# Rotating queries and keys in the projection's PSUM banks, with the order of the attention and mixing stage rewritten

## The reference

```python
h = rms_norm(x, norm1_g)
ua, qb, kb, vb, qc, kc, vc, gc = split(h @ w_in)      # 256, 3 x 512, 4 x 256 columns
ya = rms_unit(s5_mixer(ua, ...))                      # state space scan, gelu, sigmoid gate
yb = rms_unit(moba_mixer(qb, kb, vb, gq, gk, cos, sin))   # 8 heads of 64, causal softmax
yc = retention_mixer(qc, kc, vc, gc, cos, sin)        # 4 heads of 64, rotated over all 64
x = x + (concat(ya, yb, yc) * mix_out_g) @ w_out
x = x + peer_layer(rms_norm(x, norm2_g), ...)         # top 16 of 16384 experts in 8 heads
```

## Time and profile before

| | us |
|---|---|
| median of 3 runs | 957.19 |
| lowest and highest | 955.43, 958.66 |
| the profiled execution, its own time | 956.8 |
| span of the profiled execution | 955.0 |
| TensorE busy | 922.6 |
| VectorE busy | 695.2 |
| ScalarE busy | 539.0 |
| GpSimd busy | 427.1 |

### The profile page before, as it was taken

The page is one execution under the profiler, slowest core; times in us unless marked ns, Lnnn a source line. Parts: engine busy times, 40 slices in busy tenths (PEclk is TensorE's granted clock), DMA queues, the critical chain, the costliest instruction groups (busy, mean ns, idle before and its releaser), DMA issues.

```text
span 955.0 us, 20048 instructions
## 1 busy us (share of the span) xinstructions
PE 922.6 (97%) x5920; PEld 831.6 (87%) x5920; DVE 695.2 (73%) x1523; ACT 539.0 (56%) x1060; POOL 427.1 (45%) x340
## 2 busy tenths in 40 slices
PE   7797789999999999999999999999999999999998
PEld 6575578999999999999999999888888888888886
DVE  7679641107999702888888886888888888888886
ACT  7374554655554564555555555665655655565653
POOL 4583226778888888777777777100000000000000
PEclk9899799999999999999999999999999999999999
DMA  9542205045666666555565655776767767776673
GB/s 334 186 171 95 78 11 199 1 153 181 232 227 226 231 225 204 199 203 195 189 197 189 199 196 192 245 248 229 250 242 236 247 232 248 244 234 242 239 245 128
DMA packets 67739, 191.53 MB, mean 201 GB/s; under 512 B 6656, under 2 KB 8576, under 8 KB 67712
## 3 DMA queue, kind: packets, MB, share of 16 engines
q1 hardware_dynamic: 67712, 191.19, 58.8%
HBM read 173.86 MB, written 17.30 MB: 200 GB/s over the span
## 4 chain that ended last, share of the span: by engine, by line
PE 73%; POOL 11%; issue 7%; DVE 6%; ACT 2%; POOLq 0%; DMA 0%; DVEq 0%
PE ps L415 22%; PE ps L417 22%; PE ps L416 22%; POOL w_lo L1513 10%; PE ps L685 3%; DVE routing L743 2%; DVE ps L743 1%; PE ps L400 1%; ACT routing L1275 1%; POOL w_lo L1500 1%; DVE ps L894 1%; DVE small L743 0%; DVE route_t L743 0%; PE ps L407 0%; ACT w_hi L1217 0%
## 5 line engine op out<-in xcount | busy, mean ns | idle before, releaser
L1410 ACT ACTIVATE w_hi<-raw 128x512 fp32r<-128x512 f32 x512 | 308.4, 628 | 136.5 <-PE ps L417 135.7
L1513 POOL TENSOR_TENSOR w_lo<-raw,w_hi 128x512 fp32r<-128x512 f32 x256 | 327.1, 1299 | 81.3 <-ACT w_hi L1410 81.1
L415 PE MATMUL ps<-h_hi,w_hi 128*128 128x256 f32 x1088 | 308.5, 284 | 2.7 <-POOL w_lo L1513 1.4
L416 PE MATMUL ps<-h_lo,w_hi 128*128 128x256 f32 x1088 | 307.9, 283 | 0.0
L417 PE MATMUL ps<-h_hi,w_lo 128*128 128x256 f32 x1088 | 307.9, 283 | 0.0
L743 DVE TENSOR_TENSOR w_lo<-raw,w_hi 128x512 fp32r<-128x512 f32 x256 | 177.4, 693 | 56.7 <-ACT w_hi L1410 41.5
L415 PEld LDWEIGHTS ps<-h_hi,w_hi 128*128 128x128 f32 x1088 | 208.8, 192 | 3.5 <-POOL w_lo L1513 1.6
L416 PEld LDWEIGHTS ps<-h_lo,w_hi 128*128 128x128 f32 x1088 | 208.8, 192 | 0.0
L417 PEld LDWEIGHTS ps<-h_hi,w_lo 128*128 128x128 f32 x1088 | 208.8, 192 | 0.0
L415 PE MATMUL ps<-w_hi,hot_gate 128*128 128x512 f32 x512 | 199.2, 389 | 0.0
L416 PE MATMUL ps<-w_lo,hot_gate 128*128 128x512 f32 x512 | 199.2, 389 | 0.0
(11 more groups left out here) (197 smaller groups left out, 871.6 us busy)
## 6 DMA issues: line engine op xcount, KB each, us to landing
raw<-in_u_t SPq DMA_DIRECT2D x128, 512.0 KB, 3.4
raw<-in_v SPq DMA_DIRECT2D x128, 512.0 KB, 3.3
act_spill<-acts SPq DMA_DIRECT2D x62, 256.0 KB, 2.1
acts<-act_spill SPq DMA_DIRECT2D x62, 256.0 KB, 3.4
routing<-in_w_in SPq DMA_DIRECT2D x5, 2048.0 KB, 11.6
routing<-in_w_out SPq DMA_DIRECT2D x2, 2048.0 KB, 7.9
routing<-in_w_q SPq DMA_DIRECT2D x2, 2048.0 KB, 8.0
xs<-in_x SPq DMA_DIRECT2D x2, 512.0 KB, 4.3
```

The costliest lines, as they stand in the source:

```text
L415: pe.matmul(dst, s_hi, m_hi, start=first and i == 0, stop=False)
L416: pe.matmul(dst, s_hi, m_lo, start=False, stop=False)
L1410: A.activation(w_hi[:, 2 * (s % 2) + h, :], raw[:, s, h * HALF:(h + 1) * HALF], ACT.Copy)\
L1513: G.tensor_tensor(w_lo[:, slot, :], raw[:, s, h * HALF:(h + 1) * HALF], w_hi[:, slot, :].bitcast(F32), ALU.subtract).then_inc(lo_ready, 1)
```

## The change

**In PSUM.** `projected(0)` still copies the queries to SBUF; their rotation reads banks 0 and 1 and writes the rotated 16 columns into `qk`. The query's gain is folded into the cos and sin tables (`rope_q`, three small products). `projected(1)` copies the scaled keys to banks 4 and 5 instead of SBUF; squares, gain, rotation and normalisation read there, and the last multiplication writes `qk`. `projected(2)` is dropped: the retention's rotation reads banks 0 and 1, scales by `rx`, writes `ret`, and now stands in front of `states(2)`, behind a wait for slice 23.

**Waits.** Projection 2 waits for `turn_ready` 1, projection 3 also for `rot_ready`, projection 5 for `ret_rot_ready`. `drive(3)` stands in front of `late_scores(1)`, and so between slices of projection 4. `c_neg` moves behind the third scores.

**The end of the stage.** The transposes of att1's second half go through banks 4 and 5 in front of y; the first attention output also moves ahead of y. The mix parts have banks 3, 2, 4, 7, the output product has (0, 1) and (5, 6), and its first two slices start on the retention's part, ahead of `moba_mix`. The eight `keep_warm` matmuls go. On ScalarE the two lots of `exps` become one, a tiny Gelu follows them, and `root(8)`, `root(16)` come ahead of the gate's Tanh.

```diff
@@ by_slices @@
                     if k == 0 and n == 2:
-                        pe.wait_ge(turn_ready, 2)
-                    if k == 0 and n >= 3:
-                        pe.wait_ge(proj_ready, 2 * (n - 2))
+                        pe.wait_ge(turn_ready, 1)
+                    if k == 0 and n == 3:
+                        pe.wait_ge(proj_ready, 2)
+                        pe.wait_ge(rot_ready, 1)
+                    if k == 0 and n == 4:
+                        pe.wait_ge(proj_ready, 4)
+                    if k == 0 and n == 5:
+                        pe.wait_ge(ret_rot_ready, 1)
@@ TensorE's order @@
             by_slices(2, range(6, KC))
-            by_slices(3, range(0, 3))
             turn_heads(0)
-            by_slices(3, range(3, KC))
+            by_slices(3, range(0, 6))
             pe.wait_ge(states_ready, 2)
             drive(2)
-            by_slices(4, range(0, 4))
+            by_slices(3, range(6, KC))
+            by_slices(4, range(0, 1))
             turn_heads(1)
-            by_slices(4, range(4, 6))
+            by_slices(4, range(1, 3))
             late_scores(0)
+            by_slices(4, range(3, 6))
+            pe.wait_ge(states_ready, 3)
+            drive(3)
             by_slices(4, range(6, KC))
             late_scores(1)
-            by_slices(5, range(0, 2))
+            by_slices(5, range(0, 3))
...
-            by_slices(5, range(2, 4))
-            pe.wait_ge(states_ready, 3)
-            drive(3)
-            pe.wait_ge(ret_rot_ready, 1)
-            pe.wait_ge(proj_ready, 8)
+            by_slices(5, range(3, 4))
+            pe.wait_ge(proj_ready, 6)
...
+            pe.wait_ge(pT_ready, 4)
+            for b in range(2):
+                turn(4 + b, [att1[:, 4 * b + h, P:S] for h in range(4)])
+
+            pe.wait_ge(pT_ready, 6)
+            for h in range(MH):
...
+                mm = pe.matmul(ps[:, 4, c], att0[:, g // 4, g % 4, :], mv[:, 0, c], start=True, stop=True)
...
+            pe.wait_ge(ret_mix, 1)
+            transpose_mix(0)
+            out_slices(0, range(0, 2))
+            pe.wait_ge(moba_mix, 1)
+            transpose_mix(1)
+            transpose_mix(2)
             pe.wait_ge(ya_ready, 1)
...
-            keep_warm(ident, 7, 8)
...
+            out_slices(0, range(2, 6))
+            pe.wait_ge(s5_mix, 1)
+            transpose_mix(3)
+            out_slices(0, range(6, KC))
+            out_slices(1, range(KC))
@@ VectorE @@
+            def rotate(dst_, x_, m, cos, sin, turned, scales):
+
+                heads = x_[0].shape[1]
+                over = lambda a, n: a.unsqueeze(1).to_broadcast([P, heads, n])
+                for t in range(TT):
+                    did(V.scalar_tensor_tensor(turned[:, t, :, 0:m], x_[t][:, :, m:2 * m], scales[t], over(sin[:, t, 0:m], m),
+                                               ALU.mult, ALU.mult))
+                    did(V.scalar_tensor_tensor(turned[:, t, :, m:2 * m], x_[t][:, :, 0:m], scales[t],
+                                               over(sin[:, t, m:2 * m], m), ALU.mult, ALU.mult))
+                settle()
+                for t in range(TT):
+                    did(V.scalar_tensor_tensor(x_[t][:, :, 0:2 * m], x_[t][:, :, 0:2 * m], scales[t], over(cos[:, t], 2 * m),
+                                               ALU.mult, ALU.mult))
+                settle()
+                for t in range(TT):
+                    ins = tt(dst_[t], x_[t][:, :, 0:2 * m], turned[:, t], ALU.add)
...
-            step(tt(k4, k4, gain(1, 0, HD), ALU.mult))
+            k_p = psum_heads(4)
+            for t in range(TT):
+                did(tt(k_p[t], k_p[t], cols(V_GQK + HD, HD).unsqueeze(1).to_broadcast([P, MH, HD]), ALU.mult))
+            settle()
+            step(rotate([k_p[t][:, :, 0:ROPE] for t in range(TT)], k_p, half_rope, rope[:, 0], rope[:, 1], scratch(ROPE),
+                        (1.0, 1.0)))
             step(rstd_of(qk_var, 0, 32, qk_rstd))
...
-            V.tensor_scalar(c_neg, c_s, -1.0, None, ALU.mult).then_inc(c_ready, 1)
-            dve.wait_ge(c_ready, 1)
+            dve.wait_ge(half_used, 3 * KC)
+            rotate([ret[:, t, 0:2 * RW].rearrange("p (h d) -> p h d", d=HD) for t in range(TT)], psum_heads(0), HD // 2,
+                   ret_turn[:, 0], ret_turn[:, 1], scratch(HD), rx_t).then_inc(ret_rot_ready, 1)
...
             states(2)
@@ ScalarE @@
-            dst = [qk[:, :, 0:MW], qk[:, :, MW:2 * MW], ret[:, :, 0:2 * RW], ret[:, :, 2 * RW:4 * RW], mv]
+            dst = [qk[:, :, 0:MW], ps[:, 4:6, :], None, ret[:, :, 2 * RW:4 * RW], mv]
...
-            slices_high(range(16, 19))
+            slices_high(range(15, 19))
+            heads_back(0, mqT)
+            act.wait_ge(rotT_ready, 1)
             projected(1)
             square_heads(1)
...
             late_exps(0)
-            slices_high(range(34, 35))
+            projected(3)
+            slices_high(range(34, 36))
             late_exps(1)
-            projected(3)
-            slices_high(range(35, 37))
+            slices_high(range(36, 38))
...
-            exps([(att0[:, g // 4, g % 4, :], g) for g in range(4)])
-            slices_high(range(38, 39))
-            exps([(att0[:, g // 4, g % 4, :], g) for g in range(4, MH)])
-            slices_high(range(39, 40))
-            act.wait_ge(proj_ready, 8)
+            exps([(att0[:, g // 4, g % 4, :], g) for g in range(MH)])
+            A.activation(spare, quarter, ACT.Gelu_apprx_tanh)
+            act.wait_ge(proj_ready, 6)
...
+            root(8)
+            out_squares(1)
+            root(16, 8)
+            transposed_high(V_GM, 1, MIX_ORDER[0:2], MIX_BANKS, 0)
             act.wait_ge(glu_psum, 1)
             A.activation(gate_s, ps[:, 7, :], ACT.Tanh, scale=0.5).then_inc(gate_ready, 1)
-            root(8)
-            root(16, 8)
```

More of the change, by code:

```diff
@@ L288, in build @@
         std = tiny(32)
+        spare = tiny(1)
         hmax, hsum = tiny(16), tiny(16)
@@ L757, in _, with transposed_low @@
             V.memset(quarter, float(np.pi / 2)).then_inc(zeros_ready, 1)
-            def transposed_low(gain, n, order=range(KC)):
-                for i, k in enumerate(order):
+            def transposed_low(gain, n, order=range(KC), banks=range(4), first=0):
+                for i, k in enumerate(order, first):
                     dve.wait_ge(th_ready, n * KC + 2 * (i // 2) + 2)
-                    V.scalar_tensor_tensor(h_lo[:, k, :], ps[:, k // 2, (k % 2) * S:(k % 2 + 1) * S], cols(gain + k, 1),
+                    V.scalar_tensor_tensor(h_lo[:, k, :], ps[:, banks[i // 2], (i % 2) * S:(i % 2 + 1) * S], cols(gain + k, 1),
                                            h_hi[:, k, :].bitcast(F32), ALU.mult, ALU.subtract).then_inc(tl_ready, 1)
@@ L850, in _, with psum_heads, scratch @@
             dve.wait_ge(bb_ready, 1)
[L852 to L858, removed]
[L859 to L861 removed]
+            def rotate(dst_, x_, m, cos, sin, turned, scales):
[6 more added lines that the diff above has]
+                                               over(sin[:, t, m:2 * m], m), ALU.mult, ALU.mult))
+                settle()
+                for t in range(TT):
+                    did(V.scalar_tensor_tensor(x_[t][:, :, 0:2 * m], x_[t][:, :, 0:2 * m], scales[t], over(cos[:, t], 2 * m),
+                                               ALU.mult, ALU.mult))
+                settle()
+                for t in range(TT):
+                    ins = tt(dst_[t], x_[t][:, :, 0:2 * m], turned[:, t], ALU.add)
+                    if t == 0:
+                        did(ins)
+                return ins
             def by_head(a):
                 return qk[:, :, a * MW:(a + 1) * MW].rearrange("p t (h d) -> p t h d", d=HD)
+            def psum_heads(bank):
+                return [ps[:, bank + t, :].rearrange("p (h d) -> p h d", d=HD) for t in range(TT)]
+            def scratch(n, first=1024):
+                return rot_tmp[:, first:first + TT * MH * n].rearrange("p (t h d) -> p t h d", t=TT, h=MH)
+            rx_t = [rx[:, t:t + 1] for t in range(TT)]
             def head_sums(a):
@@ L932, in _ @@
                    ALU.mult))
+            half_rope = ROPE // 2
+            did(tt(rope_q[:, 0], rope[:, 0], cols(V_GQK, ROPE).unsqueeze(1).to_broadcast([P, TT, ROPE]), ALU.mult))
+            for a, b in ((0, half_rope), (half_rope, 0)):
+                did(tt(rope_q[:, 1, :, a:a + half_rope], rope[:, 1, :, a:a + half_rope],
+                       cols(V_GQK + b, half_rope).unsqueeze(1).to_broadcast([P, TT, half_rope]), ALU.mult))
             head_sums(0)
+            settle()
             q4, k4 = by_head(0), by_head(1)
-            step(tt(q4[:, :, :, 0:ROPE], q4[:, :, :, 0:ROPE], gain(0, 0, ROPE), ALU.mult))
-            rotate(q4[:, :, :, 0:ROPE], ROPE // 2, rope, rot_tmp[:, 1024:1280]).then_inc(rot_ready, 1)
+            dve.wait_ge(proj_ready, 2)
+            rotate([q4[:, t, :, 0:ROPE] for t in range(TT)], psum_heads(0), half_rope, rope_q[:, 0], rope_q[:, 1], scratch(ROPE),
```

(17 more changed lines are left out.)

142 lines of the change are left out of this document (63 added, 79 removed).

## The result

The changed kernel takes 944.54 us in the median of four runs (942.65 to 948.87), against 957.47 for the kernel before beside it: 12.9 us less, a ratio of 0.9873 with a 95% interval from 0.9836 to 0.9911. The forecast was 941.1 with a range of 935 to 949.

What follows compares the result with a forecast made beforehand. TensorE, busy 922.6 of 955.0 us, bounds the kernel; in the front VectorE's chain sets the pace. 8.3 + 2.0 + 8.7 + 2.3 - 2.7 = 18.6 us, less 2.5 for the clock: gain 16.1, 941.1 us, range 935 to 949 (own range 937 to 945).

Steps and rivals of the forecast that it cites:

- Step A: Start of projection 2: its stall and slow stretch go, `states(1)` starts at 44.5 instead of 52.78, 8.3 us gained.
- the tables and sums of q: VectorE's work between its phases and the query rotation, ahead of `states(1)`: put at 2.0 us.
- Step B: Keys on VectorE: stretch of 7.0 us instead of 12.9, `states(2)` at 66.0 against 76.33, gain 2.0 us more.
- Step C: From `states(2)` to the last projection slice: about 3.5 us new stall, end at 95.6 against 114.6, another 8.7 us gained.
- Step D: From the last projection slice to the first output slice: 23.8 us against 26.1, 2.3 gained, with a 2.6 us stall.
- the clock behind D's stall: TensorE's lower clock after the 2.6 us stall in front of the retention scores: 2.5 us lost.
- Step E: Output product: 25.5 us against 22.8, 2.7 lost, the two new table loads costed at nothing.
- Rival 1: Both new stalls have longer slow stretches behind them, small pieces and hand-overs cost more: gain 8.6, 948.6 us; chance 0.20.
- Rival 2: GpSimd is faster by some 2 us over 16 slices and the clock holds: gain 20.6, 936.6 us; chance 0.10.
- Rival 3: Gain of the early start and keys is waited away before `drive(3)` and the exponentials: under 3 us, 955 to 957; chance 0.04.
- Rival 4: TensorE stays at 1.2 GHz from `drive(3)`'s stall until the output product is done: loss 38.2, 995.4 us; chance 0.03.
- the 9 us that I had named as a sign of being wrong: On TensorE: a slow stretch longer than 9 us would show the forecast wrong.

Runs made afterwards that it cites:

- e3_keys_sbuf: Changed kernel, but the scaled keys go to SBUF and their gain, rotation and normalisation run there with the same instructions: 948.65 us, ratio 0.9917.
- e0_after: The changed kernel measured once more, nothing altered, as the mark for the other runs: 943.77 us, ratio 0.9860.
- e1: Kernel before with one edit, projection 2 waits for `turn_ready` 1 instead of 2: 948.97 us, ratio 0.9922.
- e11: Changed kernel with `turn_ready` 2 restored in front of projection 2 and the keys in SBUF: 959.53 us, ratio 1.0023.
- e2: Changed kernel with the wait for `turn_ready` 2 restored in front of projection 2: 952.27 us, ratio 0.9963.
- e5: Changed kernel with 32 small matmuls put into TensorE's stall in front of `drive(3)`: 944.87 us, ratio 0.9891.
- e4: Changed kernel with 24 small matmuls put into TensorE's stall in front of the retention scores: 945.64 us, ratio 0.9876.
- e7: Changed kernel with `drive(3)` behind `late_scores(1)` and, on ScalarE, `projected(3)` and slices 34, 35 ahead of the first exponentials: 942.57 us, ratio 0.9862.
- e6: Changed kernel with ScalarE's `projected(4)` ahead of the silu and the spare Gelu behind the last probabilities: 942.75 us, ratio 0.9844.
- e8: Changed kernel with the rearrangements of e6 and e7 together: 939.67 us, ratio 0.9828.

## Why the prediction was right, and by how much it was off

The sign and the path were right: 12.9 us where 16.1 were forecast, and 944.54 lies inside both ranges that were stated. Step by step, in the profiled execution, with its late start of 2.2 us taken off:

**Step A** (start at 44.5, 8.3 us gained): `states(1)` at 46.1, 6.6 gained. The stall went as said. What failed is the 2.0 us for "the tables and sums of q": that stretch took 3.7 us (42.63 to 46.33). The 48-element product takes 1.16 us, the three `rope_q` products, which I had put at nothing, 1.49. They have two operands in SBUF while GpSimd runs, which is the very price that step B counted for the keys and step A forgot. The same 48-element product took 0.21 us in the kernel before, where GpSimd stood still from 39.03 to 44.15 us (first line); the second is GpSimd's in the changed kernel:

```profile
40.46 0.21 DVE L743 TENSOR_TENSOR vec<-vec 128x48 f32<-128x48 f32 x1
...
39.51 5.47 POOL L1557 TENSOR_TENSOR w_lo<-routing,w_hi 128x512 fp32r<-128x512 f32 x4 [2.31 <-ACT w_hi L1270]
```

`drive(1)` was not what was waited for: its last matmul ends at 46.71 us, 1.6 us before `states(1)` starts. The early start alone is worth 7.7 us on the chip.

**Step B** (keys' stretch 7.0 us, `states(2)` at 66.0): 6.7 us, and 66.7, of which 1.6 come from A. The PSUM price of 0.69 for 512 elements was right: the group of such products in the changed kernel is

```profile
L757 DVE TENSOR_TENSOR routing<-ps,routing 128x512 f32<-128x512 f32 x10 | 6.4, 685 | 0.2
L757 DVE TENSOR_TENSOR ps<-ps,routing 128x512 f32<-128x512 f32 x6 | 4.2, 699 | 0.2
...
L757 DVE TENSOR_TENSOR ps<-ps,vec 128x512 f32<-128x512 f32 x2 | 1.3, 682 | 0.0
```

0.682 to 0.699 us. The Trainium skill (VectorE: DVE Perf Modes, section on the TRN2 errata of SBUF-source operations) has 58 fixed cycles for an SBUF source and 120 for PSUM, by my estimate 0.065 us more for PSUM. That does not show at this size: 0.686 us against 0.678. In the pair of kernels that differ in nothing else, a 64-element product takes 0.21 us from PSUM and, undisturbed, 0.21 from SBUF (61.23 us in the changed kernel, 66.54 in `e3_keys_sbuf`).

**Step C** (3.5 us of stall in front of `drive(3)`, a 3.4 us slow stretch behind it costing 1.7): 3.52 us, and a clock of 0.66 over 5 us, which is 1.7. The retention scores come at 99.9 where 99.2 was said. Up to this point the sum is off by 0.7 us. Part of that is luck: the pieces named for the stretch from `drive(3)` to the last slice add up to 19.7 us (13.7 + 4.3 + 1.7), not to the 20.4 that was written, and it took 20.5 (78.14 to 98.67).

**Step D** is the step that failed, in one term: "the clock behind D's stall", put at 2.5 out of bounds of 0 to 4.6. The trace shows 26.46 us from the retention scores to the output product and 20.87 in five profiles in which the clock did not fall. The clock so cost 5.6 us here and 4.8 in `e0_after`. Here it stood at half from 103 to about 116.7 us, in `e0_after` in two pieces of some 3.4 and 6.8 us. I had limited it to the work that I thought TensorE had to itself (5.4 us); but y and the products behind it, which I had at the full clock, ran in the same slow stretch. Without the clock the step's working (20.2 us) was short by 0.7.

**Step E** (25.5 us): 26.25, 0.75 more; two waits on ScalarE's rounding, of 0.62 and 1.49 us, stand in it where about 1.0 us was booked. (The one of 1.50 at 128.52 stands in front of it; step D had 1.4 for rounding and subtraction.) The two new table loads cost nothing, as said. ScalarE's timeline of the changed kernel:

```profile
127.06 0.84 ACT L1276 ACTIVATE h_hi<-ps,vec 128x256 fp32r<-128x256 f32 x2
127.92 1.28 ACT L1421 ACT_TABLE_LOAD   x1
129.21 0.60 ACT L1421 ACTIVATE route_t<-ps 128x512 f32<-128x512 f32 x1
```

The next activation starts 1.29 us after the load begins, and the one before ends 0.02 us ahead of it; the drain of 1.38 us that the Trainium skill adds (ScalarE: Activation LUTs, section What ACT_TABLE_LOAD costs) is not there. The other new load begins at 134.83 us, and the rounding that TensorE next waited for starts at 139.62, after ScalarE had itself been idle for 2.25 us.

**Behind the front** the forecast had TensorE's work "as before". From the warm matmuls to the end of the span it is 791.6 us in the kernel before and in `e1`, and 792.2 to 792.4 in every kernel with the new order: 0.7 us more. The cause was not looked into.

Together: 1.6 - 0.9 in A and B, 2.3 to 3.1 for D's clock, 0.7 in D, 0.75 in E and 0.7 behind it make 5.2 to 6.0 us too much by the two profiles, each of them the slowest execution of its series. The medians say 3.2, since the clock falls less in the other executions.

**The rivals.** Rival 1 (the stalls cost more) named the place and was half right: one of its two stretches came out so. Rival 2 needed GpSimd 2 us faster and a clock that holds; GpSimd's slice took 1.302 us on the page, against 1.333 before, which is 0.5 us over 16 slices. Rival 3 was refuted by `e1`. Rival 4 did not occur: the longest slow stretch was about 13.5 us. But that is over the 9 us that I had named as a sign of being wrong, and it marks the very term that failed.

What I did not see: that the gain which I booked as C and D (11.0 us) is not the new order's. By `e11` the order without early start and PSUM keys loses 2 to 3 us, clock losses taken in. The early start carries 7.7 to 8.5, the keys' operands 4.9 (7.3 with the late start, a part of it by way of the clock). I read it so that the sum held because the items of C and D were counted from the same chain, which the early start and the keys move; no run takes C or D alone.

## What to carry to other kernels

Look for waits that guard a bank nobody still uses: one such line was worth more than half of this change of many. Where VectorE works beside a busy GpSimd, read the same shape in both conditions before costing anything, and apply the price to every small operation on the path, not to the large ones alone. After a reorder, look for TensorE's new stalls and the granted clock behind them; moving the waited-for steps and filling what was left of one stall with small matmuls of its own length took another 7 us here together; filling alone gave 2 to 3.

## What the runs showed of the hardware that was not expected

The clock behind a stall is not settled by the stall's length. The 2.35 us in front of the retention scores was followed by 15 us at 0.54 in the changed kernel, and by a granted clock of 1.00 in `e2`, `e3` and `e5`, with the same stall and the same instructions behind it. In `e4` there was no stall over 0.74 us and the clock fell at 112 us. Two places of the fall can be told apart. In the changed kernel, `e0`, `e7` and `e11` it came within about 1 us of the first retention scores, right behind the stall. In `e4`, `e6` and `e8`, and once more in `e0`, it came 5 to 8 us behind these scores, after small transposes and 64-column matmuls with waits of 0.7 us between. What sets the moment stays open.

The same program's start differs with it: `states(0)` began between 27.38 and 29.62 us in these profiles, and the granted clock in 24 to 30 us was between 0.72 and 1.00. A single profile of this kernel can mislead by 2 us before the changed code even begins.
